# A new order for the front of a decoder step: rows first, norm between the factor tables, weight blocks between the rounds

## The reference, cut to what matters

```
def modulate(h, shift, scale):
    return h * (1.0 + scale[:, None, :]) + shift[:, None, :]

def split_mod(c, w, b, n):
    mod = jnp.einsum("bd,de->be", jax.nn.silu(c), w) + b
    return jnp.split(mod, n, axis=-1)

def s5_mixer(u, h0_re, h0_im, a_re, a_im, log_dt, b_re, b_im, c_re, c_im, d_skip, w_glu):
    ...
    lam_bar = jnp.exp(lam * dt)
    b_bar = ((lam_bar - 1.0) / lam)[:, :, None] * b_mat
    bu = jnp.einsum("blgp,gnp->blgn", uf.astype(jnp.complex64), b_bar)
    bu = bu.at[:, 0].add(lam_bar * h0)
    _, h = lax.associative_scan(_linear_combine, (a_seq, bu), axis=1)
    y = jnp.real(jnp.einsum("blgn,gpn->blgp", h, c_mat)) + d_skip * uf
    z = jax.nn.gelu(y.reshape(bsz, length, D_MODEL))
    ...

h = modulate(rmsnorm(x, g_norm[layer, 0]), sh1, sc1)
y, hr, hi = s5_mixer(h, ...)
```

## Time and profile before

| | us |
|---|---|
| median of 3 runs | 3589.09 (3577.5 to 3590.97) |
| span of the profiled execution | 3586.7 |
| PE busy | 2614.0 (73%) |
| DVE busy | 2357.1 (66%) |
| ACT busy | 1226.6 (34%) |
| POOL busy | 1300.8 (36%) |

### The profile page before, as it was taken

The page is one execution under the profiler, slowest core; times in us unless marked ns, Lnnn a source line. Parts: engine busy times, 40 slices in busy tenths (PEclk is TensorE's granted clock), DMA queues, the critical chain, the costliest instruction groups (busy, mean ns, idle before and its releaser), DMA issues.

```text
span 3586.7 us, 62252 instructions
## 1 busy us (share of the span) xinstructions
PE 2614.0 (73%) x24910; PEld 955.6 (27%) x24910; DVE 2357.1 (66%) x5444; ACT 1226.6 (34%) x3819; POOL 1300.8 (36%) x1153
## 2 busy tenths in 40 slices
PE   4466898867766866657879997687686668666665
PEld 2355622403200400002224666141040013001000
DVE  8653387687776677556553444878867767765645
ACT  1222232434333333335432232343433343334333
POOL 5300033444444444434422431344444344443432
PEclk7667899967866866679999999686696678667667
DMA  8756699999999999999965045999999999999997
GB/s 329 222 127 220 273 390 411 396 420 407 412 420 420 395 421 420 405 420 410 410 232 154 30 175 228 418 397 413 418 403 421 420 420 407 419 420 402 417 421 320
DMA packets 215089, 1278.54 MB, mean 356 GB/s; under 512 B 54705, under 2 KB 60313, under 8 KB 67929
## 3 DMA queue, kind: packets, MB, share of 16 engines
q0 software_dynamic: 151552, 1109.46, 75.7%
q1 hardware_dynamic: 62688, 164.77, 13.1%
q10 hardware_dynamic: 576, 0.59, 0.1%
HBM read 1260.95 MB, written 11.43 MB: 355 GB/s over the span
## 4 chain that ended last, share of the span: by engine, by line
DMA 39%; PE 33%; DVE 18%; ACT 5%; issue 3%; SPq 1%; POOL 1%; DVEq 0%; ACTq 0%; PEldq 0%; POOLq 0%
DMA arena<-peer_uv,arena 36%; PE psum L2625 11%; DVE arena L2067 8%; PE psum L2570 6%; DVE arena L1654 3%; PE psum L2531 3%; PE psum L2990 2%; DVE arena L1663 1%; PE psum L2773 1%; DMA arena<-b_mod 1%; PE psum L2704 1%; ACT arena L1372 1%; ACT arena L1369 1%; DVE arena L1985 1%; DVE arena L2078 1%
## 5 line engine op out<-in xcount | busy, mean ns | idle before, releaser
L2625 PE MATMUL psum<-arena 32*32 32x512 f32 x16384 | 1534.0, 822 | 733.5 <-ACT arena L1372 729.6
L1130 POOL DMA_INDIRECT arena<-peer_uv,arena x1040 | 1130.0, 1087 | 1943.7 <-PE psum L2625 1555.7
L2067 DVE SCALAR_TENSOR_TENSOR arena<-arena 128x1024 f32<-128x1024 f32 x1040 | 1273.0, 1226 | 762.9 <-DMA arena<-peer_uv,arena 751.1
L1359 ACT ACTIVATE arena<-arena 128x1 f32<-128x1 f32 x1040 | 210.4, 202 | 1548.5 <-DVE arena L2067 1547.7
L2625 PEld LDWEIGHTS psum<-arena 32*32 32x32 f32 x16384 | 216.3, 119 | 1913.4 <-ACT arena L1372 1819.4
L1372 ACT ACTIVATE arena<-arena 128x32 f32<-128x32 f32 x1024 | 329.0, 321 | 33.4
L1369 ACT ACTIVATE arena<-arena 128x1 f32<-128x1 f32 x1040 | 306.0, 294 | 33.8
L2570 PE MATMUL psum<-arena 128*128 128x128 f32 x2048 | 264.5, 286 | 15.8 <-DMA arena<-peer_wq 14.7
L2570 PEld LDWEIGHTS psum<-arena 128*128 128x128 f32 x2048 | 246.4, 198 | 85.2 <-issue 83.6
L2428 PE MATMUL psum<-arena 128*9 128x128 f32 x2048 | 100.2, 376 | 110.1 <-DMA arena<-b_mod 110.1
L1654 DVE TENSOR_TENSOR arena<-arena 128x512 f32<-128x512 f32 (+9 forms) x206 | 156.3, 759 | 18.6 <-ACT arena L1198 5.7
(11 more groups left out here) (315 smaller groups left out, 2282.6 us busy)
## 6 DMA issues: line engine op xcount, KB each, us to landing
arena<-w_mod SPq DMA_DIRECT2D x64, 1024.0 KB
arena<-peer_wq SPq DMA_DIRECT2D x12, 2048.0 KB, 13.0
arena<-peer_uv,arena POOLq DMA_INDIRECT x1040, 10.4
arena<-w_glu SPq DMA_DIRECT2D x5, 2048.0 KB, 12.8
arena<-mod_rows SPq DMA_DIRECT2D x4, 1024.0 KB
arena<-w_o SPq DMA_DIRECT2D x1, 4096.0 KB
arena<-mod_rows SPq DMA_DIRECT2D x7, 512.0 KB, 4.8
arena<-x_after_layer SPq DMA_DIRECT2D x7, 512.0 KB
```

What stands on the lines that cost most here:

```text
L1130: pool.indirect_dma_start(ring[r], None, a[f"peer_uv{t // 5}"], bass.IndirectOffsetOnAxis(ap=ix, axis=0)).then_inc(landed[r], 16)
L1359: act.activation(col, col, ACT.Gelu_apprx_tanh).then_inc(s_gl, 1)
L2067: dve.scalar_tensor_tensor(out=u, in0=u, scalar=1.0, in1=h, op0=ALU.mult, op1=ALU.mult, accum_out=at(DOTS + (t % 2) * 2 * P + m, 1)).then_ ...
L2625: ins = pe.matmul(acc_of(t, i, c), diag[rows, r, :], ring[r][rows, D + 512 * c:D + 512 * (c + 1)], start=(m == 0), stop=last, skip_group_c ...
```

## The change

The order of the front is new, and with it the places:

- SyncE loads the prompt rows, the gain and the samples ahead of the first weights; the S5 parameters come in two transfers.
- ScalarE sums the squares early, into PSUM. VectorE fills `bl` (POOL no longer does), then norms, then fills `cl`. Step 7 of `bl`, step 0 of `cl` and the `lamt` factors are copies of ScalarE.
- The samples' columns are made by TensorE in a new round `s` of 64 transposes and 64 products with the identity; the store and the 16 gathers fall away.
- The rounds begin after 10 blocks (`MOD_FIRST`) instead of 20. Their order is m, m, s, u, i with m, k, y; after each of twelve of them one weight block is multiplied (`MOD_AFTER`), in a single PSUM bank; blocks 22 to 31 follow after the last `k`.
- PSUM halves go by kind: `s` and `i` in the upper half, `m`, `u` and `k` in the lower, `y` in both. The injections lie six groups to a bank in three banks, and ScalarE copies them.
- The response matrices of all four rounds have places of their own; their 32 transfers are issued by POOL after block 21 and the clearing of `toep`.
- The skip product, the load of the skip row and the scan's waits move accordingly; the states are placed after the last block and after the response transfers.

```diff
+MOD_FIRST = 10
-MOD_ONE = 20
+MOD_ONE = 22
...
-        ROUNDS = ([("u", r) for r in range(NR)] + [("k", r) for r in range(NR)]
-                  + [("m", 0), ("m", 1), ("i", 0), ("m", 2), ("i", 1), ("m", 3), ("i", 2), ("i", 3)]
-                  + [("y", r) for r in range(NR)])
-        WHO = {"u": "A", "k": "A", "m": "A", "i": "V", "y": "V"}
+        ROUNDS = ([("m", 0), ("m", 1), ("s", 0)] + [("u", r) for r in range(NR)]
+                  + [("i", 0), ("m", 2), ("i", 1), ("m", 3), ("i", 2), ("i", 3)]
+                  + [("k", r) for r in range(NR)] + [("y", r) for r in range(NR)])
+        WHO = {"u": "A", "k": "A", "m": "A", "i": "A", "s": "A", "y": "V"}
+        MOD_AFTER = [("m", 0), ("m", 1), ("u", 0), ("u", 1), ("u", 2), ("u", 3), ("i", 0), ("i", 1), ("i", 2), ("i", 3),
+                     ("k", 0), ("k", 1)]
+        assert MOD_FIRST + len(MOD_AFTER) == MOD_ONE
...
+        def half_of(key):
+            kind, r = key
+            return r % 2 if kind == "y" else int(kind in "is")
+
+        def half(key):
+
+            return psum[:, 4 * half_of(key):4 * half_of(key) + 4, :]
+
+        def round_before(no):
+            mine = [key for key in ROUNDS[:no] if half_of(key) == half_of(ROUNDS[no])]
+            return mine[-1] if mine else None
+
+        def mod_between(key):
+            return divmod(MOD_FIRST + MOD_AFTER.index(key), 2)
...
-            sp.dma_start(par, a["s5_par"]).then_inc(s_par, 16)
+            sp.dma_start(par, a["s5_par"][:, 0:NPAB]).then_inc(s_par, 16)
+            sp.dma_start(at(PARC, 2 * D), a["s5_par"][:, NPAB:NPAR]).then_inc(s_parc, 16)
+            x5v = a["x_prompt"].rearrange("(c s j) d -> s c (j d)", s=2, j=TC // 2)
+            for s in range(2):
+                sp.dma_start(at(CL, 4 * D, 64 * s, 64 * s + 64), x5v[s]).then_inc(s_x5, 16)
+            sp.dma_start(at(GBC, D), a["g_norm"][0:1, :].partition_broadcast(P)).then_inc(s_mods5, 16)
+            sp.dma_start(at(XS, D, 0, NB), a["x_sample"]).then_inc(s_x5, 16)
...
+            sp.dma_start(at(SHS, D, 0, NB), mod_dram[1:NC9, 0:D]).then_inc(s_mods5, 16)
+            sp.dma_start(at(SCS, D, 0, NB), mod_dram[1:NC9, D:2 * D]).then_inc(s_mods5, 16)
             mod_loads(MOD_S5, MOD_ONE, MOD_PLACES[0])
-            sp.wait_ge(s_clr, 1)
-            sp.wait_ge(s_blp, 1)
-            for s in range(2):
-                sp.dma_start(at(U2, 4 * D, 64 * s, 64 * s + 64), x5v[s]).then_inc(s_x5, 16)
-            sp.dma_start(at(TMP, D), a["g_norm"][0:1, :].partition_broadcast(P)).then_inc(s_mods5, 16)
-            sp.dma_start(at(TMP + D, D, 0, NB), a["x_sample"]).then_inc(s_mods5, 16)
-            sp.dma_start(at(TMP + 2 * D, D, 0, NB), mod_dram[1:NC9, 0:D]).then_inc(s_mods5, 16)
-            sp.dma_start(at(TMP + 3 * D, D, 0, NB), mod_dram[1:NC9, D:2 * D]).then_inc(s_mods5, 16)
-
-            sp.wait_ge(s_h5, 2)
-            sp.dma_start(hs_dram, at(TMP + D, D, 0, NB)).then_inc(s_hst, 16)
-            sp.dma_start(mod_a, a["ssm_d"].partition_broadcast(P)).then_inc(s_dld, 16)
-            sp.wait_ge(s_hst, 16)
-            sp.wait_ge(s_tz, 2)
-            hsv = hs_dram.rearrange("b (g p) -> p g b", p=GP)
-            for b in range(NB):
-                for k, rows in enumerate((slice(0, GP), slice(P - GP, P))):
-                    sp.dma_start(u2[rows, :, CH + k * NB + b], hsv[:, :, b],
-                                 allow_slow_non_contiguous=True).then_inc(s_us, 16)
-
-            sp.wait_ge(s_tz, 1)
-            for r in range(NR):
-                wait_copied(sp, ("k", r))
-                for s in range(TC):
-                    sp.dma_start(toep[GP * s:GP * (s + 1), RG * r:RG * (r + 1), GP * s:P],
-                                 ksb[r % 2][:, :, 0:P - GP * s]).then_inc(s_toep[r], 16)
-
-            wait_copied(sp, ("i", NR - 1))
-            for r in range(NR):
-                sp.wait_ge(s_toep[r], 16 * TC)
+
+            sp.dma_start(at(ST0, 2 * HALF * NB), a["state_g"]).then_inc(s_stg, 16)
+            sp.wait_ge(s_mm, round_no[("k", NR - 1)] + 1)
+            sp.wait_ge(s_sk, 1)
             mod_loads(MOD_ONE, NMB, MOD_PLACES[1])
...
-            pool.wait_ge(s_tabs, 1)
-            shape = [P, G, GP]
-            for s in range(TC):
-                k = TC - 1 - s
-                link(pool.tensor_tensor(bl[:, :, s, :], bbar_re, ca[:, k, :].unsqueeze(2).to_broadcast(shape),
-                                        ALU.mult))
-                link(pool.tensor_tensor(tmp_g, bbar_im, bb[:, k, :].unsqueeze(2).to_broadcast(shape), ALU.mult))
-                ins = pool.tensor_tensor(bl[:, :, s, :], bl[:, :, s, :], tmp_g, ALU.add)
-                if s < TC - 1:
-                    link(ins)
-                else:
-                    ins.then_inc(s_blp, 1)
+            pool.wait_ge(s_h5, 2)
+            pool.memset(u2[:, :, CH:UC], 0.0).then_inc(s_tz, 1)
+            pool.dma_start(mod_a, a["ssm_d"].partition_broadcast(P)).then_inc(s_dld, 16)
+            wait_copied(pool, ("s", 0))
+            pool.memset(u2[96:P - GP, :, CH + NB:UC], 0.0).then_inc(s_tz, 1)
 
             for b in range(2):
                 pool.wait_ge(s_modmm[b], MOD_ONE)
             pool.memset(at(TOEP, G * P), 0.0).then_inc(s_tz, 1)
-            pool.wait_ge(s_clr, 1)
-            pool.wait_ge(s_blp, 1)
-            pool.wait_ge(s_h5, 1)
-            pool.memset(u2[:, :, CH:UC], 0.0).then_inc(s_tz, 1)
+            pool.wait_ge(s_tz, 3)
+            for r in range(NR):
+                wait_copied(pool, ("k", r))
+                for s in range(TC):
+                    pool.dma_start(toep[GP * s:GP * (s + 1), RG * r:RG * (r + 1), GP * s:P],
+                                   ksb[r][:, :, 0:P - GP * s]).then_inc(s_toep, 16)
...
+            act.wait_ge(s_x5, 48)
+            for j in range(TC // 2):
+                link(act.activation(psum[:, 0:2, :].rearrange("p b n -> p (b n)"), x5[:, j, :], ACT.Square,
+                                    accum_out=stat[:, j:j + 1]))
+            act.activation(psum[0:NB, 0:2, :].rearrange("p b n -> p (b n)"), at(XS, D, 0, NB), ACT.Square,
+                           accum_out=stat[0:NB, 4:5]).then_inc(s_sq, 1)
...
+            mod_evac(0, MOD_S5)
+            act.wait_ge(s_bb, 1)
+            act.activation(bl[0:64, :, TC - 1, :], bbar_re[0:64], ACT.Copy).then_inc(s_blp, 1)
+            act.activation(bl[64:P, :, TC - 1, :], bbar_im[64:P], ACT.Copy).then_inc(s_blp, 1)
+            act.wait_ge(s_tabs, 1)
+            for gp in range(2):
+                rows = slice(64 * gp, 64 * gp + 64)
+                for m, t in enumerate((TC, 1)):
+                    for k, (src, sign) in enumerate(((pw_re, 1.0), (pw_re, 1.0), (pw_im, -1.0), (pw_im, 1.0))):
+                        c0 = (4 * m + k) * HALF
+                        act.activation(lamt[rows, c0:c0 + HALF], src[rows, t, gp:G:2], ACT.Copy, scale=sign
+                                       ).then_inc(s_lam, 1)
             act.wait_ge(s_ms, 1)
             act.activation(stat[:, 8:13], stat[:, 8:13], ACT.Sqrt).then_inc(s_rt, 1)
+            mod_evac(MOD_S5, MOD_FIRST)
...
+                elif kind == "s":
+                    act.wait_ge(s_tz, 1)
+                    link(act.activation(u2[0:GP, :, CH:CH + NB], ps[0:GP, 0, :].rearrange("p (g b) -> p g b", g=G),
+                                        ACT.Copy))
+                    ins = act.activation(u2[96:P, :, CH + NB:UC], ps[64:96, 0, :].rearrange("p (g b) -> p g b", g=G),
+                                         ACT.Copy)
                 elif kind == "k":
-                    if r >= 2:
-                        act.wait_ge(s_toep[r - 2], 16 * TC)
-                    ins = act.activation(ksb[r % 2].rearrange("p (b g) m -> p b (g m)", b=4), ps[0:GP], ACT.Copy)
+                    ins = act.activation(ksb[r].rearrange("p (b g) m -> p b (g m)", b=4), ps[0:GP], ACT.Copy)
+                elif kind == "i":
+                    wide_i = ps[:, 0:2, 0:6 * UC].rearrange("p b (g c) -> p b g c", g=6)
+                    last_i = ps[:, 2, 0:4 * UC].rearrange("p (g c) -> p g c", g=4)
+                    for k in range(2):
+                        for gp in range(2):
+                            out = slice(64 * gp, 64 * gp + 64)
+                            src, end = wide_i[64 * k:64 * k + 64, :, gp:6:2], last_i[64 * k:64 * k + 64, gp:4:2]
+                            six, two = slice(8 * r, 8 * r + 6), slice(8 * r + 6, 8 * r + 8)
+                            link(act.activation(sj[out, :, k, six].rearrange("p c (b g) -> p b g c", b=2),
+                                                src[:, :, :, 0:CH], ACT.Copy))
+                            link(act.activation(sj[out, :, k, two].rearrange("p c g -> p g c"), end[:, :, 0:CH],
+                                                ACT.Copy))
+                            link(act.activation(si[out, k, six, :].rearrange("p (b g) c -> p b g c", b=2),
+                                                src[:, :, :, CH + NB:UC], ACT.Copy))
```

(81 more changed lines are left out.)

201 lines of the change are left out of this document (79 added, 122 removed).

## The result

The changed kernel takes 3565.54 us, the median of 5 runs (3557.36 to 3567.04), against 3589.09 (3575.16 to 3590.97, 5 runs): 23.6 us less. The ratio is 0.9938, 95% interval 0.9916 to 0.9960. The profiled execution spans 3555.2 us against 3586.7. So I read the effect of each edit at the first output product, the instant on which the prediction rests, and the time beside it. That instant is at 305.95 against 330.50: 24.5 us earlier, which is what the medians say.

A forecast was written before the change was run, and what follows sets the result against it. Everything hangs on the first output product; weight streaming and other work wait for each other. Last block's start 286.8 plus 13.6 gave 300.4 against 330.5, 30 us off the median: 3559 us, range 3530 to 3582.

The forecast's parts named there:

- the lone norm stage: Norm of the chunk rows, worked alone from 138 to 166 us; its 28 us were to leave the path whole.
- The start: Rows, gain and samples loaded ahead of the first weights: 2.65 MB at 363 GB/s, 7.3 us later.
- The rounds: From 88.5 us one weight block follows each of twelve rounds; the last response round was put near 215.
- Rival 1: TensorE stays at full clock in the mixed stage: 45 to 67 us gained, 3522 to 3544; chance 0.12.
- The sample round: New round of 64 small transposes and 64 tiny products ahead of the row turns: 12 us, between 10 and 15.
- The transfers: The 32 response transfers, issued by POOL beside the last weights: 11 us added, between nothing and 20.7.
- The injections: Four rounds at 5.5 us, each waiting for ScalarE's copy of 7.2 (5.8 to 8.2); done at 185.9.
- rival 2: Injections on ScalarE are the new bound, 14.7 us a round: 5 to 18 us gained, 3571 to 3584; chance 0.17.
- Rival 3: POOL's transfers wait for VectorE's scan, until about 260: 22 us gained to 13 lost, 3580 by the middle; chance 0.08.
- Rival 4: POOL's price for issuing 256 small runs: over 18 us slower from 3.8 us each; chance 0.06.
- Rival 5: Blocks between rounds lengthen them as much as they shorten the stream behind: about 3589 us; chance 0.04 of its own.
- nothing behind the front changes: Sign: the forecast is wrong if anything behind 330 us changes its length by more than a few us.

The follow-up runs named there:

- e1: The changed kernel without the 32 transfers that spread the response matrices; 3540.7 us (one run).
- e4: The changed kernel with chunk rows, gain and samples loaded behind the first four weight blocks instead of ahead; 3560.6 us, ratio 0.9905 to the kernel before.
- e6: The changed kernel with blocks 0 to 21 all ahead of the rounds and none between them; 3623.7 us (one run).

## Why the prediction was right

The time is 3565.5, in the range of 3530 to 3582, and 6.5 us above the 3559 that was taken; the gain is 23.6 us where 30 was forecast. The mechanism is the one forecast: the lone norm stage is gone, the blocks run among the rounds, and the last block still ends the front. The single terms were worse than their sum. At the last response round 214.6 stands against 215, but the terms up to it were off by +5.6, -5.3, +7.1, -3.8, -2.1 and -2.1, which cancel; that is luck.

| step | foreseen | measured |
|---|---|---|
| rows ahead of the weights | 7.3 | 11.6 at block 4 (60.99 - 49.39) |
| block 9 ends | 88.5 | 94.1 |
| B factors end, norm ends (hidden) | 63, 78 | 62.2, 77.5 |
| two turns, blocks 10 and 11 | 15.8 | 10.5 |
| sample round | 12 (10 to 15) | 19.1 |
| four turns of rows with blocks | 26 | 22.2 |
| first injection to the end of the fourth | 43.6 | 41.5 |
| a copy of an injection | 7.2 | 7.1 |
| from there to the last response's end | 29 | 27.0 |
| last response ends | 215 | 214.6 |
| transfers beside the weights | 11 (0 to 20.7) | 18.8; 16 to 20 by e1 |
| last block to first output | 13.6 | 11.8 (its clock 1.00, not 0.50) |
| first output product | 300.4 | 305.95 |

**The start** was mis-sized by 4.3 us. The step took the weights' 363 GB/s for all bytes; the rows move at 209 to 225, and a window of the kernel before shows that. e4 confirms the place: behind block 3 they cost 6.8 us at block 4 and not 11.6.

**The rounds** were taken with a clock between its two levels. Five of the six turns ran at 1.00 (1.94 to 1.97 us), the other turn and most of the sample round at 0.50, and the injections took 3.8, 5.7, 3.8 and 7.1 us where 5.5 was put. Rival 1, full clock through the whole mixed stage and 45 to 67 us gained, did not come: the stage had 0.82 in the mean. What spoke against it, the waits for copies, are the waits that the blocks fill (0.82 with them, 0.65 without, e6), and the clock was lost for the longest time in the sample round, where TensorE never waited.

**The sample round** is the term furthest outside its own bounds. The two prices used, a transpose of 8 rows and a bias product, were high (82 ns against 27, 76 ns against 50 a record). What was missing is that the round goes to and fro between the two kinds (e9). No row of the kernel before has such a mixture, and the bounds should have been open above for that reason.

**The transfers** were taken at half because the pace of 5.9 us a block seemed to leave gaps. It leaves few: e1 gives back 16 to 20 of the 20.7. By the table this term alone is 7.8 us, more than the 5.5 by which the first output product is late; the other terms together come to -2.3. The rule of the Trainium skill that the prediction cites (DMA: Bandwidth & Descriptors, section "Issuing engines are not separate DMA queues"), that transfers of all issuers run on the same 16 engines, was the better guide to it.

**The injections** went as reckoned, copy by copy, and rival 2's upper price was not reached. **Rival 3** is out: POOL issued all 32 transfers from 211.1 to 228.7 without a gap, 0.55 us each, while VectorE's scan ran from 214.8 on; in e6 the first 24, ahead of the scan, took 0.55 each as well. (The middle of that rival's range, 308 to 343, is 5 us gained, so 3584 and not the 3580 given; no chance hung on it.) **Rival 4** is out as well: 0.55 us each and not the 3.3 from which it would have decided; 256 short runs are cheaper to issue than a gather of 128 rows (1.1). **Rival 5** as it stands, blocks that make the rounds longer by what they save, is refuted by e6. But the rounds did get longer from another cause, which the forecast added up term by term without setting it beside the 72.6 us of the kernel before. That nothing behind the front changes holds within the scatter: 24.5 us at the first output product, 23.6 in the medians, and 3249.3 us behind it against 3256.2, both within what the other runs show.

## What to carry to other kernels

Where one stage is bound by loads and another by chains of product and copy, put the load-bound work into the waits of the chains: twelve weight blocks fitted into the rounds at no cost, and kept the clock up. But ask what the room for them cost: here rounds that wait for their own copies had first become 50 us longer. Small scattered transfers cost a full weight stream most of their engine time (16 to 20 of 20.7 us), so look for a stretch in which DMA is idle, and before work is moved out of a stage, see which waits it was filling there. Sort small TensorE work by kind, and price a load by the rate that the same load had, not by the stream's.

## What the runs showed of the hardware that I had not expected

- Going to and fro between small fp32 transposes and small fp32 products on TensorE cost 86 ns a change (128 changes, 19.1 against 8.1 us for the same instructions), at clock 0.50 about the same as at 1.00. Sorted, transposes took 27 ns for 8 x 16 (clock 1.00), and for 8 x 128 62 ns at 1.00 and 107 at 0.50; a product's record took 32 ns at 1.00 and 53 at 0.50.
- In the sample round the granted clock fell from 1.00 to 0.50 although TensorE had been busy without a gap since 102.4 us, with block 11 and then 2.7 us of small records, and stayed there for its last 16.4 us; it fell in the sorted round and in that of 71 transposes too.
- A transfer of 256 short runs within the chip took POOL 0.55 us to issue and SyncE 0.86.
- Prompt rows of 16 KB loaded to 64 partitions a transfer moved at 209 to 225 GB/s with the DMA share at 1.
